# Modulation product in 512 KB steps, half of it in the second layer, and both panels of the even output projection open together

## The reference

```python
# even layer (first): differential attention (8 heads), gated conv, memory attention
y = concatenate([ya * silu(az), yb * silu(bz), yx * silu(xz)])   # 2048 wide
h = h + y @ e_w_out
# odd layer (second): forgetting attention (12 heads), memory attention
h = h + y @ o_w_out
# second block: 12 chunks of 512 columns are 6 vectors of 1024
mod = silu(c) @ w_mod + b_mod            # w_mod is 1024 x 6144: "the modulation product"
#   the vectors: shift and scale of the mix, its gate, shift and scale of the FFN, its gate
#   the context's rows get their shift and scale from c_ctx, in the same product
mix = merge_heads(att, ret, g_r, w_out)  # on modulate(rms_norm(h), shift, scale)
ffn = (silu(a) * b) @ w_ffn_out          # a, b = split(modulated h @ w_ffn_in)
```

## Time and profile before

| | us |
|---|---|
| median of 3 runs | 1101.94 |
| lowest and highest run | 1100.93, 1110.46 |
| span of the profiled execution | 1105.6 |
| PE busy in it | 983.4 |
| DVE busy in it | 712.0 |
| ACT busy in it | 478.9 |

### The profile page before, as it was taken

One profiled execution on the slowest core, in us unless ns is written; L12 is line 12 of the kernel. 1 busy time (PEld: TensorE's weight loads), 2 busy tenths in 40 slices (PEclk: granted clock), 3 DMA queues, 4 the chain that ended last, 5 costly groups with the idle time before them and its releaser, 6 DMA issues. The chain is left out here.

```text
span 1105.6 us, 14254 instructions
## 1 busy us (share of the span) xinstructions
PE 983.4 (89%) x5508; PEld 834.2 (75%) x5508; DVE 712.0 (64%) x1038; ACT 478.9 (43%) x798; POOL 77.8 (7%) x71
## 2 busy tenths in 40 slices
PE   4999898999897999999998988987888859999996
PEld 3788776988776788989886766744567649999985
DVE  4657888887777557576877766434356466765653
ACT  4555464553324355555654343333433234353442
POOL 0201110000000002010200001000022010000000
PEclk9999998999898799999999999888989779999999
DMA  7534545655664545445546835211112216764661
GB/s 254 186 116 152 189 156 188 229 194 187 220 225 128 191 159 169 162 169 180 158 156 215 278 110 172 92 45 69 39 39 76 89 50 202 259 221 137 224 208 41
DMA packets 89413, 175.08 MB, mean 158 GB/s; under 512 B 4270, under 2 KB 8771, under 8 KB 89347
## 3 DMA queue, kind: packets, MB, share of 16 engines
q1 hardware_dynamic: 86656, 166.78, 45.1%
q0 software_dynamic: 1952, 6.77, 1.9%
q10 hardware_dynamic: 738, 0.61, 0.2%
HBM read 173.10 MB, written 1.06 MB: 158 GB/s over the span
## 5 line engine op out<-in xcount | busy, mean ns | idle before, releaser
L1468 DVE TENSOR_TENSOR wlo<-raw,whi 128x1024 fp32r<-128x1024 f32 (+2 forms) x278 | 325.0, 1183 | 165.2 <-ACT whi L1198 164.4
L1198 ACT CAST whi<-raw 128x1024 fp32r<-128x1024 f32 (+2 forms) x278 | 276.6, 1010 | 203.7 <-PE acc L932 71.8
L941 PE MATMUL acc<-xhi,whi 128*128 128x256 f32 x736 | 215.9, 293 | 9.5 <-DVE slo L1486 4.6
L942 PE MATMUL acc<-xhi,wlo 128*128 128x256 f32 x736 | 210.9, 287 | 0.0
L943 PE MATMUL acc<-xlo,whi 128*128 128x256 f32 x736 | 210.8, 286 | 0.0
L930 PE MATMUL acc<-whi,xhi 128*128 128x512 f32 (+2 forms) x368 | 151.7, 412 | 12.5 <-DVE xlo L1486 5.2
L941 PEld LDWEIGHTS acc<-xhi,whi 128*128 128x128 f32 x736 | 143.9, 196 | 13.9 <-issue 6.2
L932 PE MATMUL acc<-whi,xlo 128*128 128x512 f32 (+2 forms) x368 | 144.7, 393 | 0.0
L931 PE MATMUL acc<-wlo,xhi 128*128 128x512 f32 (+2 forms) x368 | 144.7, 393 | 0.0
L942 PEld LDWEIGHTS acc<-xhi,wlo 128*128 128x128 f32 x736 | 144.0, 196 | 0.7 <-issue 0.5
L943 PEld LDWEIGHTS acc<-xlo,whi 128*128 128x128 f32 x736 | 143.9, 195 | 0.0
(11 more groups left out here) (276 smaller groups left out, 1236.6 us busy)
## 6 DMA issues: line engine op xcount, KB each, us to landing
raw<-in_e_w_in SPq DMA_DIRECT2D x28, 1024.0 KB, 5.2
raw<-in_o_w_in SPq DMA_DIRECT2D x28, 1024.0 KB, 5.0
raw<-in_w_mod SPq DMA_DIRECT2D x24, 1024.0 KB, 5.2
raw<-in_w_ffn_in SPq DMA_DIRECT2D x20, 1024.0 KB, 5.2
raw<-in_w_in SPq DMA_DIRECT2D x14, 1024.0 KB, 5.2
raw<-in_w_ffn_out SPq DMA_DIRECT2D x10, 1024.0 KB, 5.1
raw<-in_e_w_out SPq DMA_DIRECT2D x8, 1024.0 KB, 6.7
raw<-in_o_w_out SPq DMA_DIRECT2D x8, 1024.0 KB, 5.1
```

What stands on the lines that cost most here:

```text
L941: mm(o, wh, hi, start=a, stop=False, skip_group_check=True)
L942: mm(o, wl, hi, start=False, stop=False, skip_group_check=True)
L1198: nc.scalar.copy(whi[:, s.i % SPLIT_SLOTS, 0:s.nk, 0:n], raw[:, s.raw.i % RAW_SLOTS, s.koff:s.koff + s.nk, 0:n]).then_inc(S["hi_ready"], 1)
L1468: tt(wlo[:, slot, 0:s.nk, 0:n], raw[:, s.raw.i % RAW_SLOTS, s.koff:s.koff + s.nk, 0:n], whi[:, slot, 0:s.nk, 0:n].bitcast(F32), ALU.subtra ...
```

## The change

The modulation product goes in steps of one k, from loads of two k tiles (512 KB) in place of four; a chunk of eight k has four loads. A chunk's steps stand `stride` rows apart and its output at pos + 8 x stride, one row behind the last step (the product steps have rank 3, behind a head's steps of the same row). The chunks 0 to 3 have stride 2 and lie in rows 28 to 94 of the even layer. The chunks 6 to 9 move to the second layer, to rows 112 to 147, with stride 1. 4 and 5 lie in rows 152 to 169, 10 and 11 in 216 to 233. There are 188 raw loads in place of 164. In DVE's part each step waits for the `mod_read` of the step before it in place of a link between the instructions of one chain, and `mod_bias` waits for the chunk's last `mod_read`. The even output projection opens both panels and alternates between them. Lines below the change move by a few numbers: L1468 becomes L1473, L1678 L1683, L1687 L1689, L896 L901.

```diff
+MODK = 2
...
-    def mod(self, pos, chunk, ctx=False, gate=False):
-        pos = max(pos, self.pos) + max(pos, self.pos) % 2
-        def read(u, part):
...
+    def mod(self, pos, chunk, ctx=False, gate=False, stride=1):
+        pos = max(pos, self.pos)
+        def read(k):
...
-            st = self.step("mod", chunk=chunk, u=u, part=part, ctx=ctx)
+            st = self.step("mod", chunk=chunk, u=k // MODK, part=k % MODK, ctx=ctx, prev=self.count.get("mod_read", 0))
...
-                st = self.step("mod_bias", chunk=chunk)
+                st = self.step("mod_bias", chunk=chunk, mod_read=self.count["mod_read"])
...
-        for i in range(4):
-            self.at(pos + (i if ctx else i // 2 * 2), lambda i=i: read(i // 2, i % 2))
-        self.at(pos + 6, out, 2)
-        return pos + 8
+        for k in range(KT):
+            self.at(pos + k * stride, lambda k=k: read(k), 3)
+        self.at(pos + KT * stride, out, 2)
+        return pos + KT * stride + 1
...
-    for chunk in (6, 7, 8, 9, 0, 1, 2, 3):
-        m = pl.mod(m, chunk, ctx=chunk < 4)
+    for chunk in range(4):
+        m = pl.mod(m, chunk, ctx=True, stride=2)
...
-    for c in range(2):
-        pl.panel("e_w_out", c * CW, CW, "y", "resid", kts=EVEN_Y // P, c=c, order=[(0, 8), (12, 16), (8, 12)])
+    outs = [pl.panel("e_w_out", c * CW, CW, "y", "resid", kts=EVEN_Y // P, c=c, opened=True) for c in range(2)]
+    for c, a, e in ((0, 0, 8), (0, 12, 16), (1, 0, 8), (0, 8, 12), (1, 8, 16)):
+        pl.parts(outs[c].panel, a, e)
...
     b = heads("X", "g1", evs, pl.pos, 4, 12, gain="ox")
+    m = max(m, b)
+    for chunk in range(6, 10):
+        m = pl.mod(m, chunk)
...
-                mod_load = Load(len(raws), "w_mod", st.u * RAWK * P, RAWK, st.chunk * CW, CW, None)
+                mod_load = Load(len(raws), "w_mod", st.u * MODK * P, MODK, st.chunk * CW, CW, None)
...
             def mod(st):
                 raw_wait(dve, st.raw)
-                half = RAWK // 2
-                for k in range(st.part * half, st.part * half + half):
-                    for v in range(2 if st.ctx else 1):
...
+                wait(("mod_read", st.prev))
+                k = MODK * st.u + st.part
+                src = raw[:, st.raw.i % RAW_SLOTS, st.part, :]
+                for v in range(2 if st.ctx else 1):
...
+                ins.then_inc(S["mod_read"], 1)
             def mod_bias(st):
                 wait(("bias_in", 16 * st.on["bias_in"]))
+                wait(("mod_read", st.mod_read))
```

More of the change, by code:

```diff
@@ L377, in load @@
         return st
-    def mod(self, pos, chunk, ctx=False, gate=False):
-        pos = max(pos, self.pos) + max(pos, self.pos) % 2
-        def read(u, part):
-            if u == 0 and part == 0 and gate:
+    def mod(self, pos, chunk, ctx=False, gate=False, stride=1):
+        pos = max(pos, self.pos)
+        def read(k):
+            if k == 0 and gate:
                 st = self.step("mod_bias_in", chunk=chunk, prev=self.count.get("mod_ps", 0))
                 self.tick(st, "bias_in")
-            st = self.step("mod", chunk=chunk, u=u, part=part, ctx=ctx)
+            st = self.step("mod", chunk=chunk, u=k // MODK, part=k % MODK, ctx=ctx, prev=self.count.get("mod_read", 0))
             self.tick(st, "mod_read")
@@ L1669, in mod @@
                 raw_wait(dve, st.raw)
-                half = RAWK // 2
-                for k in range(st.part * half, st.part * half + half):
-                    for v in range(2 if st.ctx else 1):
[L1673 to L1683, removed]
+                wait(("mod_read", st.prev))
+                k = MODK * st.u + st.part
+                src = raw[:, st.raw.i % RAW_SLOTS, st.part, :]
+                for v in range(2 if st.ctx else 1):
+                    c = scol[:, 8 * v + k:8 * v + k + 1]
+                    if k == 0:
+                        ins = ts(macc[:, v, :], src, c, None, ALU.mult)
+                    else:
+                        ins = stt(macc[:, v, :], src, c, macc[:, v, :], ALU.mult, ALU.add)
+                ins.then_inc(S["mod_read"], 1)
             def mod_bias(st):
                 wait(("bias_in", 16 * st.on["bias_in"]))
+                wait(("mod_read", st.mod_read))
                 tt(macc[0:1, 0, :], macc[0:1, 0, :], macc[0:1, 1, :], ALU.add).then_inc(S["bias_done"], 1)
```

## The result

The changed kernel takes 1178.13 us (median of 4 runs, 1175.85 to 1179.60) against 1103.45 for the kernel before, run beside it. The ratio is 1.0655, 95% interval 1.0612 to 1.0698. The forecast was 1143 us with a range of 1098 to 1168: slower, as forecast, but by 75 us and not by 41, and outside the range.

The account below looks back on a forecast made before the run. PE was taken as the bound, with its idle time and lowered clock to be won or lost. The terms summed to 1105.6 - 28 + 55 + 15 = 1147.6, less 3.7, rounded down to 1143 us; range 1098 to 1168.

Parts of the forecast that it names:

- Step 1: Even layer: four chunks leave, the rest spread out and panels are freed earlier, saving 28 us (bounds 0 and -51).
- Step 2: DMA queue: 24 more loads, 3.7 us per 512 KB, are hidden and cost 0 as bandwidth, but each takes a whole slot.
- Step 3: Second layer, output projection, FFN: laps (product step, load, cast, `wlo`) make PE wait at eight outputs, +55.3 us (bounds 0, 102).
- Rival C: Second layer: DVE's head chains come late behind the laps, so PE waits for them too; 1165 us; chance 0.18 with D.
- Step 4: PE's granted clock falls after four long and four short stalls: +15 us (bounds 0 and 30).
- A: Second layer: free DVE time and splits made ahead cover the laps, the even layer's gain remains; 1077 us; chance 0.15.
- B: Eight outputs: DVE keeps up with the laps, only the output's distance of about a row costs; about 1105 us; chance 0.12.
- D: Even layer: no gain, its idle is head chains; sign PE idle still above 20 us; 1163 us; 0.18 with Rival C.

Follow-up runs that it names:

- e3: The changed kernel with the raw ring cut into six slots of two k tiles in place of three of four, all loads 512 KB: 1106.5 us.
- e7: The changed kernel with the product of chunks 0 to 3 left out save for its first k tile: 1156.5 us.
- e8: The kernel before with the raw ring in six slots of two k tiles and all loads 512 KB, steps and order as before: 1090.2 us.
- e1: The changed kernel with chunks 6 to 9, 4, 5, 10 and 11 each starting at an odd row: 1159.9 us.
- e11: The same plan as e10, but in six slots of 512 KB: 1091.8 us.
- e2: The changed kernel with the outputs of chunks 6 to 9, 4, 5, 10, 11 two rows further behind the last product step: 1156.9 us.
- e10: The changed kernel, all chunks but 0 to 3 in the before kernel's grain, chunks 6 to 9 in rows 96 to 126, three 1 MB slots: 1144.2 us.
- e9: The changed kernel with six ring slots and the outputs of the stride-1 chunks two rows later: 1099.4 us.

## Why the prediction was wrong

**What bounds the kernel: right.** PE, with idle time and clock as what can be gained or lost.

**Step 1, the even layer: this is the step that failed.** I put it at -28 us; it measured -7.5. The forecast was 1147.6 for the span, and 1176.2 was measured: 28.6 us more, of which 20.5 are here and 8.8 in rows 112 to 240: idle time 2.5, clock 0.5, and 5.8 for the moved output matmuls, for which I had no term. (In the even layer the same line took 13.9 us before and 10.1 after, so 3.8 of the 7.5 gained are only moved too.) (The medians differ by another 5.6, since this kernel's profiled span lies 1.9 us under its median and that of before 3.7 over.) By the forecast's two halves:

```
rows      forecast  after   e3 (six slots)  e7 (product left out)
28-62     -8        +4.0    +3.5            -3.1
62-96     -20       -11.5   -19.2           -23.1
```

In rows 28 to 62 the sign was wrong. Six slots change nothing there and leaving the product out gives 7.1 us, so what costs is DVE's product steps, two vectors of each k in the same rows, and not the ring. The size of -8 was taken from the window's idle time and clock without asking what their absence gives: 3.1. And the output of chunk 0 brought a wait of its own:

```profile
189.97 1.20 PE L1058 MATMUL opsum<-cst,macc 128*128 128x1 f32 x5 [5.10 <-DVE ytok L1661]
...
341.26 0.80 PE L935 MATMUL acc<-whi,shi 128*128 128x512 f32 x1 [4.78 <-DVE xlo L1491]
```

It stands behind a head whose result DVE has yet to take out of the same bank (`opsum`, `ytok`). e7, with hardly any product, waits 5.29 us there too, so it is the place of the output and not the product steps; no run moves it. The second row is the wait at the transposes in row 84, 2.1 us before and in e7.

In rows 62 to 96 the sign was right, and with six slots the -20 is there. In three slots the step "the DMA waits of the cast there go" is false: ACT's wait for e_w_out is 22.2 us, where it was 24.9. I had counted how many rows ahead each slot comes free (three for panels, two for modulation loads). What counts is the time. DVE, SP and ACT in the even output projection of the kernel after:

```profile
280.68 1.22 DVE L1473 TENSOR_TENSOR wlo<-raw,whi 128x1024 fp32r<-128x1024 f32 x1
281.81 1.41 DVE L1683 SCALAR_TENSOR_TENSOR macc<-raw,scol,macc 128x512 f32<-128x512 f32 x2
...
283.24 0.37 SPq L901 DMA_DIRECT2D raw<-in_w_mod  x1
283.66 2.23 SPq L901 DMA_DIRECT2D raw<-in_e_w_out  x2
294.63 0.37 SPq L901 DMA_DIRECT2D raw<-in_w_mod  x1
295.04 2.23 SPq L901 DMA_DIRECT2D raw<-in_e_w_out  x2
...
289.84 1.99 ACT L1203 CAST whi<-raw 128x1024 fp32r<-128x1024 f32 x2 [7.50 <-DMA raw<-in_e_w_out]
301.22 2.00 ACT L1203 CAST whi<-raw 128x1024 fp32r<-128x1024 f32 x2 [6.74 <-DMA raw<-in_e_w_out]
```

The panel load's slot is free at 281.90, when the `wlo` ends, and ACT is ready for the cast at 282.34, 0.4 us later. So nearly the whole load shows as a wait, 6.2 us from the issue at 283.66 to the cast. Only 1.8 us come from the queue: SP issues in order, and the load stands behind a modulation load that waits for the product step. The laps of this stretch take 11.4 us for four rows (289.84 to 301.22), and PE needs 11.2 for four bare rows, so the casts' waits hardly reach it: PE's own wait for a `wlo` in rows 28 to 97 fell from 8.0 to 2.4 us.

So of the missing 20.5 us, 8.5 are in rows 62 to 96, and six slots give 7.7 of them back. The other 12.0 are in rows 28 to 62: 7.1 go with the product steps (e7), and 4.9 were not there even without them.

**Step 2, the 512 KB loads: right.** As bandwidth they cost nothing (e8, e3). One took 3.9 us in the changed kernel, where I used 3.7. The estimate from the page of the Trainium skill ("DMA: Bandwidth & Descriptors", Anatomy of one DMA), which is for another DMA path, was 3.2. The measured figure decides, and it is 0.7 us longer.

**Step 3, the laps: right in mechanism, and in its sum partly by luck.** The waits were forecast at 55.3 us and PE's idle time grew by 57.8 in these rows; with the clock I had 70 us and the trace has 73, besides the moved matmuls. A lap measured 8.2 and 9.3 us against 8.5, and chunk 10 cost +11.8 against +11.6. But the other terms miss both ways. PE's waits at the outputs of chunks 6, 8 and 4 were 6.6, 10.7 and 7.6 us; the forecast was 9.1, 11.9 and (8.1 and the 3.2 of before) 11.3. Chunk 5's was 8.3 for 3.5, chunk 11's 4.7 for 3.1, and rows 143 and 144 took 10.3 where all of chunk 9 was put at 5.6. I had let DVE catch up after each long wait, and e1 shows that leads of two rows run late too. Rival C's sign, waits for a head's steps, is small: 3.3 us for a `ptb` (2.1 before), 1.7 for a `ytmp`, 1.4 for a `qkT`.

**Step 4, the clock: right.** Forecast +15, measured 15.5 in those rows, 0.27 us for each us of added idle (15.5 / 57.8). I had taken 2.5 us for each of four long waits and 1.2 for each of four short ones, which is 0.27 for each of the 55.3 as well.

**The rivals.** A (faster, 1077) fell: three laps in a row are not covered. Its rule from the Trainium skill ("Perfetto Trace Analysis", Optimizing Scalar/DVE Operations), that breaking up instructions may complete work sooner, is not borne out here. In three slots each smaller piece took a whole slot, and in six the kernel with the pieces (e11) is no faster than the one without (e8). B (distance only, 1105) fell by e2 and e3. C and D gave 1163 to 1165, nearest to the truth. D, that the even layer does not gain, is most of what happened (its sign, over 20 us idle there, is met with 24.8); C is not. I gave them 0.18 together, and let the range end where one of them alone would end, with nothing left for the other terms' errors.

## What to carry to other kernels

When loads are made smaller, look at what they occupy and not at what they transfer: in a ring of fixed slots a half-size load takes a whole slot's place in the queue. Here sixteen of them in place of eight full ones cost 21 us in the rows of four chunks (e10 against the kernel before), and cutting the same memory into twice as many slots of half the size took 52 and 72 us off the kernels with such loads and 16 off the one without.

Count a load's lead in time, from the end of the instruction that frees its slot to the moment the cast could begin, and not in rows; then add what it waits behind others in the issuing queue (1.8 us here). And put a ceiling on a saving by the run or the stretch in which the work is absent, before taking it from a stage's whole idle time.

## What the runs showed that was not expected

In six slots a 512 KB load took 4.2 to 4.7 us in the five largest groups and up to 6.3 in a small one (3.9 in the changed kernel, 3.7 in the earlier trace rows), and yet the casts hardly waited: being early was worth more than being quick. The low clock took 0.27 us for each us of idle that the change added; but in the even layer's window from 250 us on it stayed at 0.89 though the idle time there fell from 15.9 to 11.2 us. And a chunk that spilled into the second block's first rows cost 10 to 13 us there (e2, e9), most of it one wait of 7.9 us at its output: the same output that costs nothing three rows behind its last step in one place waits for a norm's evacuation in another.
